# Gated delta layer of a two-block layer stack: five stages become one interleaved stage, and the triangular inverses of two layers work on packed 64-wide blocks

## The reference, cut to what matters

```python
def _chunk_gated_delta_rule(q, k, v, g, beta):
    ...
    gc = jnp.cumsum(chunks(g[..., None])[..., 0], axis=-1)
    k_beta, v_beta = k * beta, v * beta
    ...
    decay = jnp.exp(jnp.where(causal, gc[..., :, None] - gc[..., None, :], -jnp.inf))
    L = jnp.where(strict, jnp.einsum('bhnid,bhnjd->bhnij', k_beta, k) * decay, 0.0)
    ...
    tinv = lax.linalg.triangular_solve(eye + L, jnp.broadcast_to(eye, L.shape), left_side=True, lower=True)
    u_c = tinv @ v_beta
    w_c = tinv @ (k_beta * jnp.exp(gc)[..., None])
    a_intra = jnp.where(causal, jnp.einsum('bhnid,bhnjd->bhnij', q, k) * decay, 0.0)
    ...
    def step(S, inp):
        q_i, k_i, u_i, w_i, a_i, gl = inp
        v_new = u_i - w_i @ S
        o = q_i @ S + a_i @ v_new
        S = S * gl[..., None, None] + jnp.einsum('bhck,bhcv->bhkv', k_i, v_new)
        return S, o
```

## Time and profile before

| | us |
|---|---|
| three runs | 5255.11, 5265.63, 5267.5; median 5265.63 |
| the profiled execution: its own time, its span | 5256.64, 5254.9 |
| its mean granted TensorE clock | 0.896 of full speed |
| `rwkv_rec`, from its first inverse product to the first product of the next stage | 291.9 to 828.3 |
| GDN, from the first product of `gdn_low` to the end of `gdn_turn_y` | 1743.7 to 2079 |
| busy over the whole span | PE 80%, PEld 50%, DVE 32%, ACT 12%, POOL 12% |

### The profile page before, as it was taken

How to read it: one execution, slowest core, us unless ns; L and a number is a source line. 1 busy time by engine, 2 the same in 40 slices (tenths; PEclk the granted TensorE clock), 3 DMA queues, 4 the chain that set the end, 5 groups by cost and what they waited for, 6 DMA issues and landing times. The chain is left out here.

```text
span 5254.9 us, 48413 instructions
## 1 busy us (share of the span) xinstructions
PE 4188.9 (80%) x19143; PEld 2616.8 (50%) x19143; DVE 1672.8 (32%) x2770; ACT 643.9 (12%) x1222; POOL 633.9 (12%) x470
## 2 busy tenths in 40 slices
PE   5999996999898485899989754767774988667774
PEld 2588883444346484344436643434442766434442
DVE  6656643420243644200132265210003124310003
ACT  2211111000112121100011100000001013100000
POOL 0133321000101240100000141100001004200001
PEclk9999997999998797999999877889996998789997
DMA  3211202542120001122122001389993200389996
GB/s 114 72 61 37 82 24 82 202 158 79 57 75 22 0 0 45 59 70 92 56 73 80 9 0 58 119 331 401 401 402 134 80 32 1 116 328 401 402 400 231
DMA packets 243056, 707.73 MB, mean 135 GB/s; under 512 B 22140, under 2 KB 117812, under 8 KB 192084
## 3 DMA queue, kind: packets, MB, share of 16 engines
q1 hardware_dynamic: 223172, 662.03, 33.9%
...
## 5 line engine op out<-in xcount | busy, mean ns | idle before, releaser
L2505 PE MATMUL experts_pg<-moe_wg,experts_xt 128*64 128x256 f32 x4224 | 520.1, 409 | 142.0 <-DMA moe_wg<-in_moe_w_up 126.8
L86 PE MATMUL ffn_in_ps<-ut,ffn_in_ring 128*128 128x512 f32 x1408 | 612.6, 595 | 25.6 <-DMA ffn_in_ring<-in_ffn_w_in 25.6
L2505 PEld LDWEIGHTS experts_pg<-moe_wg,experts_xt 128*64 128x64 f32 x4224 | 330.5, 148 | 314.6 <-issue 157.2
L86 PEld LDWEIGHTS ffn_in_ps<-ut,ffn_in_ring 128*128 128x128 f32 x1408 | 266.4, 190 | 362.2 <-issue 335.8
L465 PE MATMUL ffn_out_y<-ffn_out_ring,ffn_h 128*128 128x512 f32 x704 | 307.7, 599 | 20.4 <-DMA ffn_out_ring<-in_ffn_w_out 20.4
L2520 PE MATMUL experts_py<-moe_wd,experts_ht 128*64 128x512 f32 x1056 | 258.1, 633 | 41.8 <-DVE experts_ht L2572 24.3
L86 PE MATMUL att_proj_ps<-att_proj_ring,ut 128*128 128x512 f32 x576 | 249.2, 596 | 18.3 <-DMA att_proj_ring<-in_attn_w_qkv 18.3
L2570 DVE TENSOR_TENSOR experts_h<-experts_hs,experts_pg 128x256 f32<-128x256 f32 x66 | 27.8, 421 | 649.5 <-ACT experts_hs L2539 649.5
L465 PEld LDWEIGHTS ffn_out_y<-ffn_out_ring,ffn_h 128*128 128x128 f32 x704 | 135.0, 193 | 190.3 <-issue 168.2
L86 PEld LDWEIGHTS att_proj_ps<-att_proj_ring,ut 128*128 128x128 f32 x576 | 177.7, 309 | 89.6 <-DMA att_proj_ring<-in_attn_w_qkv 18.7
L573 DVE TENSOR_TENSOR ffn_h<-ffn_in_act_out,ffn_in_ps 128x512 f32<-128x512 f32 x44 | 30.3, 688 | 531.8 <-ACT ffn_in_act_out L560 531.8
...
## 6 DMA issues: line engine op xcount, KB each, us to landing
...
```

The source lines that it names most:

```text
L86: last = nc.tensor.matmul(out, lhsT, rhs, start=(i == 0), stop=(i == len(pairs) - 1))
L2505: last = nc.tensor.matmul(pg[ch * SLOTS:(ch + 1) * SLOTS, b, side, 0:HH], xt[:, b, kk % MQ, kk // MQ, :], wg[:, b, side, kk, ch * HH:(ch + ...
```

## The change

**In both inverses** levels 0 to 5, which never leave the two 64x64 diagonal blocks, run on packed tiles: the upper block of a head lies in partitions 0 to 63, the lower one in 64 to 127, and the four heads take 256 columns, not 512. Each 128x128x128 matmul becomes two of 64x64x64, one in each diagonal quarter of the array, that write the same PSUM bank at different partitions. Level 6, which joins the two blocks, is one 64x64x64 matmul a head on `cross`, the block below the diagonal. The result goes to a full-width tile `inv`. POOL, ACT and DVE touch 256 columns where they touched 512. Only level 6's DVE and POOL work changes kind: POOL has none, DVE copies.

**In GDN** one stage, `gdn_rec`, replaces the five. It has the form of `rwkv_rec`: a head of four items of `low` work, one buffer each, then iterations 0 to 4, in which the slots hold the scan of the two items before, the `low` work of item n+4, and the norm, gate and transposes of finished chunks. `yt` now lies in `kq[:, :, 1, :]`.

The diff, cut; the loops over the levels in GDN are those shown for RWKV. Indentation that all lines share is left out.

```diff
-ITEMS, GR, LEVELS, W = NC * 4, 4, 7, 4 * P
+ITEMS, GR, LEVELS, HB = NC * 4, 4, 7, P // 2
...
-src = st.sb("src", [P, 2, 2, W])
+src, cross = st.sb("src", [P, 2, 2, W]), st.sb("cross", [HB, 2, 2, W])
+inv = st.sb("inv", [P, 2, 2, 4 * P])
+level, eye = st.sb("level", [P, LEVELS - 1, HB]), st.sb("eye", [P, HB])
...
-                    m = k.level[:, lv:lv + 1, :].to_broadcast([P, 4, P])
+                    m = level[:, lv:lv + 1, :].to_broadcast([P, 4, HB])
...
                     if lv:
                         pe.wait_ge(s["t_joined"], 12 * i + 2 * (lv - 1) + h + 1)
                     for q in range(4):
-                        last = nc.tensor.matmul(px[:, h, q * P:(q + 1) * P], ltm[:, h, lv % 2, q * P:(q + 1) * P],
-                                                t[:, h, q * P:(q + 1) * P] if lv else k.ident[:, :], start=True, stop=True)
+                        cols = slice(q * HB, (q + 1) * HB)
+                        if lv < LEVELS - 1:
+                            for b in blocks:
+                                last = nc.tensor.matmul(px[b, h, cols], ltm[b, h, lv % 2, cols], t[b, h, cols] if lv else eye[b, :],
+                                                        start=True, stop=True)
+                        else:
+                            last = nc.tensor.matmul(px[blocks[1], h, cols], cross[:, i % 2, h, cols], t[blocks[0], h, cols],
+                                                    start=True, stop=True)
                     last.then_inc(s["x_made"], 1)
                 slot(i, 2 * lv)
...
+                            for b in blocks:
+                                last = nc.tensor.matmul(px[b, h, cols], tt_[b, h, cols], lx[b, h, cols], start=True, stop=True)
                         last.then_inc(s["z_made"], 1)
                     for q in range(4):
-                        last = nc.tensor.matmul(pzt[:, h, q * P:(q + 1) * P], lx[:, h, q * P:(q + 1) * P],
-                                                tt_[:, h, q * P:(q + 1) * P], start=True, stop=True)
+                        cols = slice(q * HB, (q + 1) * HB)
+                        if lv < LEVELS - 1:
+                            for b in blocks:
+                                last = nc.tensor.matmul(pzt[b, h, cols], lx[b, h, cols], tt_[b, h, cols], start=True, stop=True)
+                        else:
+                            last = nc.tensor.matmul(pzt[blocks[0], h, cols], lx[blocks[1], h, cols],
+                                                    inv[blocks[1], i % 2, h, q * P + HB:(q + 1) * P], start=True, stop=True)
                     last.then_inc(s["zt_made"], 1)
...
+                cols = slice(side * 2 * HB, (side + 1) * 2 * HB)
+                for b in blocks:
+                    nc.vector.copy_predicated(p2(src[b, par, h, cols]), mask[b, 0:1, b].to_broadcast([HB, 2, HB]),
+                                              p2(ps[b, first + side, 0:2 * P])[:, :, b])
+                last = nc.vector.tensor_copy(p2(cross[:, par, h, cols]), p2(ps[blocks[0], first + side, 0:2 * P])[:, :, blocks[1]])
             last.then_inc(s["low_taken"], 1)
...
-                                            ALU.add).then_inc(s["joined"], 1)
+                    if lv < LEVELS - 2:
+                        nc.vector.tensor_tensor(tt_[:, h, :], tt_[:, h, :], pzt[:, h, 0:W], ALU.add).then_inc(s["joined"], 1)
+                    elif lv == LEVELS - 2:
+                        for b in blocks:
+                            last = nc.vector.tensor_tensor(q4(inv[b, i % 2, h, :])[:, :, b], q4(tt_[b, h, :]), q4(pzt[b, h, 0:W]), ALU.add)
+                        last.then_inc(s["joined"], 1)
+                    else:
+                        nc.vector.tensor_copy(q4(inv[blocks[0], i % 2, h, :])[:, :, blocks[1]],
+                                              q4(pzt[blocks[0], h, 0:W])).then_inc(s["joined"], 1)
                 slot(i, 2 * lv + 1)
...
-        with Stage(nc, "gdn_rec") as rec:
-ITEMS = NC * 2
...
-with Stage(nc, "gdn_low") as st:
...
-inverse_stage(nc, k, "gdn_inv", lt, ITEMS)
-with Stage(nc, "gdn_scan") as st:
...
-rms_gate_stage(nc, k, "gdn_out", y, z, TT * H, HW, 1e-6, a["gdn_norm_g"][0], at)
-transpose_stage(nc, k, "gdn_turn_y", [([y[:, tt, (half * 4 + q) * P:(half * 4 + q + 1) * P] for q in range(4)],
...
+        for n in range(4):
+            decays(n)
+        pool.wait_ge(s["compact"], 4)
+        for i in range(N):
...
+                if lv in (1, 5) and i and 2 * (i - 1) + (lv == 5) + 4 < ITEMS:
+                    decays(2 * (i - 1) + (lv == 5) + 4)
...
+        def low(n):
+            c, tc = n // 2, chunk(n // 2)
+            for q in range(4):
+                nc.tensor.matmul(ps[:, A, q, :], g[:, c, head(n, q):head(n, q) + 1].to_broadcast([P, P]), k.causal[:, 1, :], start=True, stop=True)
+            for q in range(4):
+                nc.tensor.matmul(ps[:, B, q, :], beta[:, c, head(n, q):head(n, q) + 1].to_broadcast([P, P]), k.ident[:, :], start=True, stop=True)
+            for q in range(4):
+                last = nc.tensor.matmul(ps[:, C_ + q // 2, (q % 2) * 2:(q % 2) * 2 + 2, :], kq[:, head(n, q), 0, tc],
+                                        kq[:, head(n, q), :, tc], start=True, stop=True)
+            last.then_inc(s["low_made"], 1)
+
...
+            if phase == 1:
+                if n >= 4:
+                    pe.wait_ge(s["turn_taken"], (n - 4) // 2 + 1)
+                if n + 4 < ITEMS:
+                    low(n + 4)
+            if phase == 3:
+                pe.wait_ge(s["low_taken"], min(ITEMS, n + 5))
                 for q in range(4):
...
+            if phase == 4:
+                for q in range(4):
+                    nc.tensor.matmul(ps[:, B, q, :], kq[:, h0 + q, 0, chunk(c)], state[:, h0 + q, :], start=True, stop=True)
...
+            if phase == 5:
+                pe.wait_ge(s["rhs_done"], n + 1)
+                pe.wait_ge(s["joined"], 14 * (n // 2) + 12 + n % 2 + 1)
+                for q in range(4):
...
+            if phase == 6:
+                pe.wait_ge(s["tok_taken"], n + 1)
+                pe.wait_ge(s["u_taken"], n + 1)
+                for q in range(4):
...
+        for n in range(4):
+            if n:
+                pe.wait_ge(s["low_taken"], n)
+            low(n)
...
+        def take_low(n):
+            par, h = (n // 2) % 2, n % 2
+            dve.wait_ge(s["dmasked"], n + 1)
+            for half in range(2):
+                pv = ps[:, C_ + half, :, :].rearrange("p (q w) t -> p q w t", q=2)
+                dm = dmask[:, :, half * 2:half * 2 + 2, :]
+                cols = slice(half * 2 * HB, (half + 1) * 2 * HB)
+                p2 = lambda ap: ap.rearrange("p (q t) -> p q t", q=2)
+                for b in blocks:
+                    nc.vector.scalar_tensor_tensor(p2(src[b, par, h, cols]), pv[b, :, 0, b], -1.0, dm[b, 0, :, b], ALU.mult, ALU.mult)
+                nc.vector.scalar_tensor_tensor(p2(cross[:, par, h, cols]), pv[blocks[0], :, 0, blocks[1]], -1.0,
...
+                step(nc.vector.tensor_tensor(at[:, n, half * 2:half * 2 + 2, :], pv[:, :, 1, :], dm[:, 1, :, :], ALU.mult))
+            for b in blocks:
+                nc.vector.tensor_tensor(q4(src[b, par, h, :]), q4(src[b, par, h, :]), ps[b, B, :, b], ALU.mult)
+            nc.vector.tensor_tensor(q4(cross[:, par, h, :]), q4(cross[:, par, h, :]), ps[blocks[0], B, :, blocks[1]],
+                                    ALU.mult).then_inc(s["low_taken"], 1)
...
+            if phase == 1 and n + 4 < ITEMS:
+                arguments(n + 4)
+            if phase == 2:
+                if n + 4 < ITEMS:
+                    take_low(n + 4)
+                if n >= 2 and n % 2 == 0:
+                    squares((n - 2) // 2)
+            if phase == 3 and n >= 2 and n % 2 == 0:
+                gates((n - 2) // 2)
+            if phase == 3 and n >= 3 and n % 2 == 1:
+                normal((n - 3) // 2)
+            if phase == 4:
...
+        for n in range(4):
+            arguments(n)
+            take_low(n)
```

440 lines of the change are left out of this document (288 added, 152 removed).

## The result

The changed kernel takes 5113.82 us (median of 4 runs, 5111.30 to 5118.88), the kernel before 5266.02 beside it: ratio 0.972, 95% interval 0.970 to 0.973. The forecast was 5133. The profiled execution took 5118.9 us against 5256.6, 138 less. By stretches of the two traces: the first product behind RWKV's stage (`rwkv_norm`) comes at 756.1 us instead of 828.3, 72 earlier; from GDN's first `low` product to the first of the output projection (its stage is `gdn_norm2` in the code) it is 271.1 us instead of 343.0, 72 less; all stages that the change doesn't touch are together some 6 us longer.

What follows compares the result with a forecast made beforehand. It took TensorE to bound RWKV's iterations (DVE iteration 0), and GDN's five stages each their own limit with exposed waits. RWKV 81 plus GDN 52 gave 133 us less, 5133 us; range 5075 to 5200.

Steps and rivals of the forecast that it cites:

- A packed product, 0.46 us: Both inverses: sixteen 64x64 MATMULs at 0.029 us each take 0.46 us, against 0.89 for a full-array product.
- TensorE's work, -13.5 us an iteration: RWKV: products take 16.7 us instead of 32.0, less 1.8 for shape changes, so TensorE's work falls 13.5 to 47.
- the term of 1.8 us for shape changes: RWKV: nine more changes between tile shapes an iteration, at 0.2 us each, cost 1.8 us.
- RWKV, -11 in each of seven iterations: RWKV's iterations 1 to 7: each 11 us shorter, 77 us together, within the stage's 81.
- I give 2.5 us an iteration back: RWKV: DVE's long blocks ahead of additions PE waits for take back 2.5 us of each iteration's saving.
- Two marks it had set for being wrong: RWKV: a granted clock below 0.8, or DVE always busy with iterations of 55 us, would make the prediction wrong.
- the 283: GDN's new stage, head through end: pieces summing to 283 us, 52 less than before; bounds 242 and 318.
- No overlap: Rival, both inverses: a pair's tiles run one after the other, a product stays 0.93 us; about 5260, 6%.
- Issue at 0.06: Rival, packed products: instructions issue one by one at 0.06 us, a product takes 0.99; about 5290, 2%.
- Interleaving gains nothing: Rival, GDN: the `low` chain and DVE's blocks add up to the old 335 us, RWKV gains 81; 5185, 12%.
- More is hidden: Rival: RWKV gives all of PE's saving and GDN comes to 242; some 190 us less, 5075, 12%.
- The clock falls: Rival, both stages: small tiles and broken-up work lower TensorE's clock; 28% at the lower level cancels 133 us; 6%.

Runs made afterwards that it cites:

- e11: The changed kernel with 14 more copies of 128x256 on VectorE in each RWKV iteration, read by nobody; 5122.41 us, ratio 0.973.
- e4b: The kernel before with GDN interleaved but its inverse on full 128x128 tiles, in a buffer of its own; 5202.26 us, ratio 0.988.
- e5: The changed kernel with GDN's head working on two items at a time through the inverse's idle banks; 5089.72 us, ratio 0.966.
- e7: The changed kernel with GDN's head working on two items at a time and later taking of items inside the iterations; 5077.97 us, ratio 0.966.

## Why the prediction was right, point by point

**A packed product, 0.46 us.** Right: 0.46 to 0.47, and the tiles overlap in one bank. The section Restrictions and Gotchas of TensorEngine Tiling (Array Packing) in the Trainium skill has different row tiles unable to use one PSUM bank at the same time; here a pair, whose two tiles differ in rows and in columns, starts every 0.058 us in one bank, as often as single tiles do at level 6, and the measurement decides. Two tiles with different rows and the same columns in one bank were not tried.

**TensorE's work, -13.5 us an iteration.** By length and clock it is 15.4 at the upper level. That is the 15.3 of the products alone, so the term of 1.8 us for shape changes was mis-sized. There are indeed ten more changes an iteration in the trace. But the 0.14 and 0.21 us that the prediction read run from the start of one MATMUL to the start of the next, and the sum had already counted the usual spacing, 0.03 or 0.11, as part of the product: a change adds some 0.1 us, about 1 us an iteration in all. The same holds after: the last MATMUL of a packed product starts at 437.57, the full tile at 437.72, 0.15 us for a spacing of 0.03. Why even this 1 us isn't seen in the 15.4 stays open; TensorE's idle time fell by only 0.2 us an iteration.

**RWKV, -11 in each of seven iterations.** -9.4: 423.8 us before, 357.8 after. The step that failed is "I give 2.5 us an iteration back" to DVE's blocks: TensorE was idle 1.4 us an iteration before and 1.2 after, not more, it is busy 98% where "some 90%" was forecast, and in `e11` 5.5 us more of DVE's work cost 0.8 us. In its place stands the clock, about 6 us an iteration, which the prediction had only as a rival that decides the sign, and took the earlier trace rows to speak against. The loss to the clock (6) was larger than the loss given to DVE (2.5), the gain on TensorE (15.4) larger than the 13.5 counted, so the term came out near for a reason that was partly wrong: that is luck. Two marks it had set for being wrong, a clock below 0.8 and iterations of 55 us, were touched (0.79 in iteration 7, 55.4 us in iteration 4) without the forecast falling.

**Iteration 0 and the start.** -12.4 instead of -7, since DVE's 42.65 us fell to 30.37. The start +5.4 (first inverse product 297.3 instead of 291.9) instead of +3. Iteration 8 and the end +0.9.

**GDN.** 263 us from the first product to the norm's first weight load where 283 stood: head 52.4 (58), iteration 0 22.0 (25), iterations 1 and 2 56.7 (56) and 58.2 (64), 3 and 4 37.7 and 26.5 (42, 27), end 10 (11). The places of the waits were right. TensorE waited ahead of L1730 for 3.90, 5.28, 4.04 and 5.28 us, where 5 to 6 stood, and 1.2 an item ahead of phase 5's products (L1742) where 1 stood. The whole stage was 20 us shorter than the 283. Mis-sized were the head, 14.3 an item for 13.1, and the norm of chunk 0, 8 us in iteration 2: it added 1.5. In 58.2 us DVE was busy 35.5, so the passes most likely filled time in which it had waited.

**The sum.** RWKV gave 72 us where 81 stood and GDN 72 where 52 stood. The two errors are of opposite sign, and by luck they leave a total that is 19 us from the forecast.

**The rivals.** No overlap: out by the 0.46 us and the row of level 6. Issue at 0.06: out by 0.029. Interleaving gains nothing: out by `e4b`, where it takes 53.5 us off alone. More is hidden: in part, 20 us in GDN, and `e5` to `e7` show that another 40 were there. The clock falls: true in kind, at an estimated 38 us in six iterations, where the rival needed 133 in all to turn the sign.
